# 128-row scores in the forgetting attention, and the low part of every weight formed on VectorE

## The chip, the cores and the metric

The program runs on one core of one Trainium2 chip. The metric is the device time of one execution in microseconds (us); lower is better. Engines are called by the profile's names: PE is TensorE's matmul, PEld its weight load, DVE is VectorE, ACT ScalarE, POOL GpSimd, SP the queue that starts most transfers.

## The reference

One sequence of 512 tokens with 1024 features goes through four layers, all in float32.

- **a**: RMS norm, then a mixer of two halves: a gated three-tap convolution (512 features), and *forgetting attention* with 8 heads of 64: softmax of `q k / 8 + C[t] - C[s]` over the keys s up to t, where C is the running sum of `log_sigmoid` of one gate value per head and token. Output projection, norm, residual, SwiGLU feed-forward (FFN, hidden size 2816), norm, residual.
- **b**: a conformer convolution module (pointwise, 31-tap depthwise, layer norm, SiLU, pointwise), then the same FFN.
- **c**: an HGRN2 mixer (gated linear recurrence, 8 heads of 128), then a FFN whose gate first passes a three-tap convolution.
- **d**: grouped-query attention over a window of 128 keys with sinks, 16 heads of 64, then the FFN with the convolution, and a final norm.

```
log_f = jax.nn.log_sigmoid((proj[..., OFF_F:] + b_f).astype(jnp.float32))
y_b = forgetting_attention(q, k, v, log_f).reshape(bsz, seq, D_FOX)
return jnp.concatenate([y_a, y_b.astype(h.dtype)], axis=-1) @ w_out
```

## The kernel before

Activations lie feature-major: 8 chunks of 128 features by 512 tokens. All weights come as 378 *slots* of 128x1024 float32 (512 KB) through a ring of 4 buffers (`RING`), in the order of `SLOT_PARTS`. A product is made of three matmuls in the float32r type (`product`): each weight and each activation is split into a high part, rounded to float32r, and a low part, the rest; high by high, high by low and low by high are added in PSUM. One slot is 8 products, so 24 matmuls of 512 columns.

For each slot: SP loads `raw` when the buffer is free (`slot_done` of the slot 4 before); ACT copies it to `w_hi` (`high_part`, called through `slot_over(s)`, which waits until slot s is done and makes the high part of slot s+3, as `AHEAD = 3`); POOL subtracts, `w_lo = raw - w_hi` (`low_part`, L396), and raises `w_ready`; PE waits for `w_ready` to reach the slot's number plus one. The low parts are made in slot order. POOL also does 6 of the 8 products of the four post-norms (`norm_output`), the blocks of depthwise taps (`tap_blocks`) and 3 chunks of the last norm; the low parts fill the rest of its list. Every engine works through its own list in order; semaphores are the only tie.

The places that matter here:

- **Start of a stage after a norm** (`a_pre`, `b_pre`, `c_pre`, and the four `*_fpre` at a FFN): PE runs `two_chunks` (slots s0, s0+1 at once, chunk by chunk as `u_lo` arrives), then slot s0+2, then `mean_square`, whose result ACT turns into `rs`, the factor by which all outputs of the stage are scaled (`rs_ready`), and without a wait for `rs` PE goes on with slot s0+3.
- **`norm_add`** on DVE (L1401, L1411, L1393) after the post-norms of layers a and b: residual adds `h`, low parts `u_lo` of the new inputs, then `sum_squares` (L1388).
- **`feed_forward`** on DVE, `pair(i, b)`: scale the gate output by `rs` (L1475), in layers c and d wait for ACT (L1047) and add two taps (L1485), then wait for the value slot and ACT's SiLU, multiply, scale, and split into `hid_hi` and `hid_lo`. One pair goes with two slots.
- **Forgetting attention** (`scores`, `attend`, L636 to L664): for each of 8 heads PE makes the scores of 4 query blocks, one or two slots of the gated convolution (`conv_slot`, 12 slots in 8 heads; even heads have one, odd heads two), all but the last two of the last slot's 8 products; then transposes of the probabilities, those last two products, and the values (plain float32, L662, a pass of 2 instructions each), whose output has 64 rows. Two heads share one bank, and ACT and DVE split it once for two heads. ACT's list per head: 4 exps, high parts, 4 copies of the transposes; DVE's: 4 maxima (L1560), reciprocal, 4 scalings (L1567), then the convolution's work.
- **Window attention** (layer d): scores have a 128-row contraction already, low and high part of a query in the two halves of the rows (`dq`). DVE's list per head pair: normalise (L1910), query low part (L1860), maxima (L1891), output low part, query evacuation, next pair's mask and add (L1881).

Of the kernel before, what the change touches and what calls it, by code (L numbers as in the profile page):

```python
# [5 lines left out]
F32 = mybir.dt.float32  # L6
# [6 lines left out]
P = 128  # L13
# [6 lines left out]
FOX_HEADS, FOX_DIM = 8, 64  # L20
HG_HEADS = 8
# [94 lines left out]
def build(nc, weights, vectors, squares, select_d, masks_d, x_t, out_t):  # L116
    with ExitStack() as ctx:
# [29 lines left out]
        with ExitStack() as fox:  # L147
            aq_hi = sb("aq_hi", [P, 4, T], F32R, fox)
            aq_lo = sb("aq_lo", [P, 4, T], F32R, fox)
            ak_hi = sb("ak_hi", [P, 4, T], F32R, fox)  # L150
            ak_lo = sb("ak_lo", [P, 4, T], F32R, fox)
            av = sb("av", [P, TT, 512], F32, fox)
            az = sb("az", [P, T + SHORT_TAPS - 1], F32, fox)
            agc = sb("agc", [P, T], F32, fox)
            ay = sb("ay", [P, T], F32, fox)
# [5 lines left out]
            ac = sb("ac", [FOX_HEADS, T], F32, fox)  # L161
# [3 lines left out]
            select = sb("select", [P, FOX_HEADS, P], F32R, fox)  # L165
# [48 lines left out]
        STAT, TOK_STAT = bank[4], bank[5]  # L214

# [54 lines left out]
        def rows_of(e):  # L270
            return slice(64 * e, 64 * e + 64)

# [120 lines left out]
        def _(pool):  # L393
            def low_part(s, j):
                pool.wait_ge(hi_ready, s + 1)
                pool.tensor_tensor(w_lo[:, j, :], raw[:, j, :], w_hi[:, j, :].bitcast(F32), ALU.subtract)\  # L396
                    .then_inc(w_ready, 1)

            def low_parts(a, b):

                if b - a >= RING:
                    with pool.Fori(0, (b - a) // RING) as i:
                        for n in range(RING):
                            low_part(RING * i + a + n, (a + n) % RING)
                for s in range(b - (b - a) % RING, b):
                    low_part(s, s % RING)

# [16 lines left out]
            pool.wait_ge(w_ready, DVE_SLOTS)  # L424
            low_parts(DVE_SLOTS, SLOT["a_ffn_in"] + AHEAD - 1)
            norm_output("a_post")
            low_parts(SLOT["a_ffn_in"] + AHEAD - 1, SLOT["b_in"] + AHEAD - 1)
            norm_output("a_fpost")
            low_parts(SLOT["b_in"] + AHEAD - 1, SLOT["b_in"] + AHEAD)

            pool.memset(bwv[:, :, :], 0.0).then_inc(taps_zeroed, 1)
            for n in range(2 * KC):
                s = SLOT["b_in"] + AHEAD + n
                low_part(s, s % RING)
                if n == 1:
                    pool.wait_ge(taps_landed, 16 * SHIFTS * (GROUPS + 1))
                if 1 <= n <= CONV_RING:
                    tap_blocks(n - 1)
                if n % 2 and n // 2 >= CONV_RING:
                    tap_blocks(n // 2)  # L440
            low_parts(SLOT["b_out"] + AHEAD, SLOT["b_ffn_in"] + AHEAD - 1)
            norm_output("b_post")
            low_parts(SLOT["b_ffn_in"] + AHEAD - 1, SLOT["c_fq"] + AHEAD - 1)
            norm_output("b_fpost")
            low_parts(SLOT["c_fq"] + AHEAD - 1, N_SLOTS)
# [7 lines left out]
        def _(pe):  # L453
# [184 lines left out]
            def scores(hd):  # L638
                r, c = slice(64 * (hd % 2), 64 * (hd % 2) + 64), hd // 2
                for qb in range(TT):  # L640
                    w = (qb + 1) * P
                    if hd > 0:
                        pe.wait_ge(pt_ready, 4 * hd)
                    s = bank[4 + qb]
                    product(s[:, 0:w], aq_hi[r, c, qb * P:w], aq_lo[r, c, qb * P:w], ak_hi[r, c, 0:w], ak_lo[r, c, 0:w],
                            True, False)
                    pe.matmul(s[:, 0:w], select[:, hd, :], ac2[:, 0:w], start=False, stop=False)  # L647
                    pe.matmul(s[:, qb * P:w], ident_r[:, :], causal[:, :], start=False, stop=True).then_inc(scores_ready, 1)

            def attend(hd, between):  # L650
                r = slice(64 * (hd % 2), 64 * (hd % 2) + 64)
# [12 lines left out]
                last.then_inc(o_ready, 1)  # L664
# [16 lines left out]
            pe.wait_ge(qkl_ready, 8)  # L681
# [9 lines left out]
            def fox_ready(k):  # L691
                if k < 4:
                    pe.wait_ge(u_ready, SPLIT["a_gate"] + k + 1)
                else:
                    pe.wait_ge(ol_ready, k - 3)
# [266 lines left out]
        def _(act):  # L962
# [136 lines left out]
            for dst, src in ((ident_r[:, :], ident), (causal[:, :], ap[:, 0, 0:P]), (select[:, :, :], select_raw)):  # L1099
# [3 lines left out]
            for n in range(8):  # L1103
# [3 lines left out]
                act.activation((aq_hi if n < 4 else ak_hi)[:, n % 4, :], ut[:, n % 2, :], ACT.Copy).then_inc(qkh_ready, 1)  # L1107
# [19 lines left out]
            for hd in range(FOX_HEADS):  # L1127
# [15 lines left out]
                for kt in range(TT):  # L1143
                    act.wait_ge(pt_full, 4 * hd + kt + 1)
                    after(act, o_ready, hd)
                    act.activation(apt[:, kt, kt * P:T], bank[4 + kt][:, kt * P:T], ACT.Copy).then_inc(pt_ready, 1)
                conv_over(slots[-1])
                if hd % 2:
                    act.wait_ge(o_ready, hd + 1)
                    act.activation(acat_hi[:, 4 + hd // 2, :], bank[3][:, :], ACT.Copy).then_inc(oh_ready, 1)  # L1150
# [219 lines left out]
        def _(dve):  # L1370
            def split_value(name, c, make):
# [58 lines left out]
            def keep_out(part, stat, bias=None):  # L1430
                for n in range(KC):
                    dve.wait_ge(slot_done, SLOT[part] + n + 1)
                    keep_chunk(stat, n, bank[n % 4], bias(n) if bias else None)

            def add_out(l):

                for n in range(KC + 1):
# [5 lines left out]
                    if n >= 2:  # L1443
                        sum_squares(f"{l}_fpre", (n - 1,))

            def add_ffn(l, stat, split=None):

                for half in range(2):
                    for n in range(4 * half, 4 * half + 4):
# [580 lines left out]
```

## Time and profile before

| | |
|---|---|
| median of 3 runs | 2493.75 us (2493.46 to 2494.15) |
| the profiled execution: its time | 2494.29 us |
| its span in the trace | 2492.5 us |
| mean granted PE clock | 0.983 of full |
| busy: PE, DVE, POOL, ACT | 2406.4, 1266.8, 1001.1, 822.3 us |
| POOL low parts (L396) | 376, 936.4 us |

The span is the stretch from the first to the last instruction; the time of an execution is 1.8 us longer. Busy time is the union of an engine's instructions; PE's matmuls overlap in it, since each is shown longer than the distance to the next one. A wait is named by the instruction that ended it.

### The profile page before, as it was taken

What the parts mean: (1) busy time and instruction counts of PE and PEld (TensorE: products, weight loads), DVE (VectorE), ACT (ScalarE), POOL (GpSimd) and SP (SyncE); (2) the same over time, 40 slices, a digit from 0 to 9 for tenths busy, and PEclk for the clock granted to TensorE, in tenths of its full rate; (3) what the DMA queues carried; (4) which work ended last, traced back from release to release, by engine and by line L of the source; (5) the groups of instructions that cost most, each with busy time, mean ns of one, the idle gap of its engine ahead of it and who ended that gap; (6) DMA issues with size and microseconds to landing.
All of it is one profiled execution on the core that took longest, in us unless ns stands there. A gap on an engine that the chain in (4) does not pass through costs nothing.

```text
span 2492.5 us, 30910 instructions
## 1 busy us (share of the span) xinstructions
PE 2406.4 (97%) x11202; PEld 1922.7 (77%) x11202; DVE 1266.8 (51%) x1590; ACT 822.3 (33%) x1194; POOL 1001.1 (40%) x416
## 2 busy tenths in 40 slices
PE   8999899999899889999989999999999979999997
PEld 6777688888664678888768888888888768888886
DVE  4453544411533464441166776577731796677701
ACT  5333422222321532222242254333322564332322
POOL 3223444444543344444443222454444313444543
PEclk9999999999899999999989999999999999999999
DMA  4112233333264223333322211333333212333332
GB/s 152 60 51 69 67 101 93 101 93 93 62 168 121 68 76 93 99 95 93 93 72 85 60 43 51 94 101 93 101 93 93 77 36 68 93 101 93 97 97 77
DMA packets 68001, 216.12 MB, mean 87 GB/s; under 512 B 11600, under 2 KB 12112, under 8 KB 67920
## 3 DMA queue, kind: packets, MB, share of 16 engines
q1 hardware_dynamic: 67632, 214.63, 28.8%
q8 instruction: 56, 0.92, 0.1%
q10 hardware_dynamic: 288, 0.36, 0.1%
q14 instruction: 25, 0.20, 0.0%
HBM read 210.64 MB, written 4.33 MB: 86 GB/s over the span
## 4 chain that ended last, share of the span: by engine, by line
PE 91%; DVE 5%; ACT 1%; issue 1%; POOL 1%; DMA 0%; DVEq 0%; SPq 0%; POOLq 0%
PE bank L456 28%; PE bank L457 27%; PE bank L458 27%; PE bank L718 2%; PE bank L811 2%; DVE ds L1910 1%; DVE h L1411 1%; DVE u_lo L1393 1%; PE bank L662 1%; ACT ds L1327 1%; PE bank L647 0%; DVE small L1891 0%; PE bank L655 0%; POOL m L413 0%; DVE dq L1860 0%
## 5 line engine op out<-in xcount | busy, mean ns | idle before, releaser
L396 POOL TENSOR_TENSOR w_lo<-raw,w_hi 128x1024 fp32r<-128x1024 f32 x376 | 936.4, 2496 | 1446.1 <-ACT w_hi L971 1446.0
L456 PE MATMUL bank<-u_hi,w_hi 128*128 128x512 f32 x1952 | 773.4, 396 | 19.1 <-DVE u_lo L1393 18.7
L457 PE MATMUL bank<-u_lo,w_hi 128*128 128x512 f32 x1952 | 766.2, 393 | 0.0
L458 PE MATMUL bank<-u_hi,w_lo 128*128 128x512 f32 x1952 | 765.9, 392 | 0.0
L971 ACT ACTIVATE w_hi<-raw 128x1024 fp32r<-128x1024 f32 x378 | 395.0, 1056 | 999.9 <-PE bank L458 929.9
L456 PEld LDWEIGHTS bank<-u_hi,w_hi 128*128 128x128 f32 x1952 | 370.8, 190 | 106.8 <-DVE u_lo L1393 23.6
L458 PEld LDWEIGHTS bank<-u_hi,w_lo 128*128 128x128 f32 x1952 | 370.4, 190 | 78.1
L457 PEld LDWEIGHTS bank<-u_lo,w_hi 128*128 128x128 f32 x1952 | 371.1, 190 | 76.6 <-issue 1.0
L456 PE MATMUL bank<-hid_hi,w_hi 128*128 (+1 forms) x704 | 278.1, 395 | 0.0
L458 PE MATMUL bank<-hid_hi,w_lo 128*128 (+1 forms) x704 | 278.1, 395 | 0.0
L457 PE MATMUL bank<-hid_lo,w_hi 128*128 (+1 forms) x704 | 278.1, 395 | 0.0
L1494 DVE TENSOR_SCALAR hid_hi<-ut 128x512 f32 (+1 forms) x88 | 203.2, 2309 | 11.8 <-DVE ut L1491 0.3
L1489 DVE TENSOR_TENSOR ut<-gconv,bank 128x512 f32<-128x512 f32 x88 | 60.6, 689 | 225.9 <-PE bank L458 190.8
L458 PEld LDWEIGHTS bank<-hid_hi,w_lo 128*128 128x128 f32 x704 | 132.0, 187 | 32.4
L456 PEld LDWEIGHTS bank<-hid_hi,w_hi 128*128 128x128 f32 x704 | 132.0, 187 | 32.3
L457 PEld LDWEIGHTS bank<-hid_lo,w_hi 128*128 128x128 f32 x704 | 132.0, 187 | 32.2
L1496 DVE TENSOR_TENSOR hid_lo<-ut,hid_hi 128x512 f32 (+1 forms) x88 | 140.3, 1595 | 10.1
L1426 DVE COPY m<-bank 128x512 f32<-128x512 f32 x24 | 16.5, 688 | 249.4 <-ACT sq L986 240.6
L1047 ACT ACTIVATE gconv<-ut,vec 128x512 f32<-128x512 f32 x44 | 36.0, 818 | 236.1 <-DVE ut L1475 236.1
L1451 DVE TENSOR_TENSOR h<-h,bank 128x512 f32<-128x512 f32 x16 | 11.0, 688 | 200.8 <-PE bank L458 200.2
L1485 DVE SCALAR_TENSOR_TENSOR gconv<-ut,vec,gconv 128x511 f32<-128x511 f32 x88 | 66.1, 751 | 55.2 <-ACT gconv L1047 49.3
L1388 DVE TENSOR_TENSOR acc<-acc,sq 128x512 f32<-128x512 f32 x73 | 77.9, 1067 | 7.6 <-ACT sq L986 4.6
(271 smaller groups left out, 2463.7 us busy)
## 6 DMA issues: line engine op xcount, KB each, us to landing
raw<-weights_dram SPq DMA_DIRECT2D x378, 512.0 KB, 3.5
bz<-gated_dram SPq DMA_DIRECT2D x32, 270.0 KB, 5.0
gated_dram<-bz SPq DMA_DIRECT2D x8, 272.0 KB, 2.1
h<-x_t_dram SPq DMA_DIRECT2D x8, 256.0 KB, 5.9
out_dram<-m SPq DMA_DIRECT2D x8, 256.0 KB, 2.2
ap<-select_dram SPq DMA_DIRECT2D x1, 512.0 KB, 8.7
vec<-vectors_dram SPq DMA_DIRECT2D x1, 343.0 KB, 7.7
cmask<-masks_dram ACTq DMA_DIRECT2D x1, 224.0 KB, 2.6
```

Of the source, the lines that this page charges most:

```text
L396: pool.tensor_tensor(w_lo[:, j, :], raw[:, j, :], w_hi[:, j, :].bitcast(F32), ALU.subtract)\
L456: pe.matmul(out, wh, xh, start=start, stop=False)
L457: pe.matmul(out, wh, xl, start=False, stop=False)
L458: return pe.matmul(out, wl, xh, start=False, stop=stop)
L718: last = pe.matmul(out[32 * g:32 * g + 32, :], bw[:, b, g * STEPS + q, :], bz4[:, b, g, SHIFTS * q:SHIFTS * q + T], start=(q == 0), stop=( ...
L811: last = pe.matmul(out, ck[:, hd, s], queries, start=True, stop=True)
L971: act.activation(w_hi[:, j, :], raw[:, j, :], ACT.Copy).then_inc(hi_ready, 1)
L1388: dve.tensor_tensor(acc[:, :], sq[:, 0, :] if c == 1 else acc[:, :], sq[:, c % 2, :], ALU.add).then_inc(acc_ready, 1)
L1485: dve.scalar_tensor_tensor(out=gconv[:, b, back:], in0=ut[:, b, 0:T - back], scalar=w, in1=gconv[:, b, back:], op0=ALU.mult, op1=ALU.add). ...
L1489: dve.tensor_tensor(ut[:, b, :], gconv[:, b, :], bank[2 * b + 1][:, :], ALU.mult).then_inc(ht_ready, 1)
L1494: dve.tensor_scalar(hi, ut[:, b, :], 1.0, None, ALU.mult).then_inc(hh_ready, 1)
L1496: dve.tensor_tensor(lo, ut[:, b, :], hi.bitcast(F32), ALU.subtract).then_inc(hid_ready, 1)
```

## The change

1. **Scores with 128 rows.** Before, a head's query and key parts (`aq_hi`, `aq_lo`, `ak_hi`, `ak_lo`) lay in 64 rows and the scores took three 64-row matmuls; the forget term (`select`) and the causal mask were two more of 128 rows. Now `aq` holds a head's high part in its own 64 rows and the low part in the other 64; `ak_hi` holds the high key part in both halves, and `ak_lo` the low key part in the head's rows and zeros in the others. Two 128-row matmuls give the three products. ACT makes 2 instead of 1 pieces for each query slot and 4 instead of 1 for each key slot, DVE 2 instead of 1, and DVE writes the zeros. `select` is one column per head, broadcast.
2. **Values in two halves of the rows.** The output of query blocks 0 and 3 goes to one half of the bank's rows, that of blocks 1 and 2 to the other (`FOX_HALVES`), 7 matmuls per head instead of 4. ACT and DVE now split each head's output in two pieces of 64 rows by 256, and the values of a head wait for the split of the head before.
3. **All low parts on DVE.** POOL makes none. DVE makes slots 0 to 2 at the start, and every later one in `low_over(s)` (slot s+3), at places in its own list.
4. `agc`, `ay`, `ac` take the memory of `sq` and `acc`.

```
-            def low_part(s, j):
-                pool.wait_ge(hi_ready, s + 1)
-                pool.tensor_tensor(w_lo[:, j, :], raw[:, j, :], w_hi[:, j, :].bitcast(F32), ALU.subtract)\
-                    .then_inc(w_ready, 1)
...
+            def low_part(s, i=0):
+                j = s % RING
+                dve.wait_ge(hi_ready, s + RING * i + 1)
+                dve.tensor_tensor(w_lo[:, j, :], raw[:, j, :], w_hi[:, j, :].bitcast(F32), ALU.subtract).then_inc(w_ready, 1)
+            def low_over(s, i=0):
+                if s + AHEAD < N_SLOTS:
+                    low_part(s + AHEAD, i)
...
scores(hd):
-                    product(s[:, 0:w], aq_hi[r, c, qb * P:w], aq_lo[r, c, qb * P:w], ak_hi[r, c, 0:w], ak_lo[r, c, 0:w],
-                            True, False)
-                    pe.matmul(s[:, 0:w], select[:, hd, :], ac2[:, 0:w], start=False, stop=False)
+                    pe.matmul(s[:, 0:w], aq[:, c, e, qb * P:w], ak_hi[:, c, e, 0:w], start=True, stop=False)
+                    pe.matmul(s[:, 0:w], aq[:, c, e, qb * P:w], ak_lo[:, c, e, 0:w], start=False, stop=False)
+                    pe.matmul(s[:, 0:w], select[:, hd:hd + 1].to_broadcast([P, P]), ac2[:, 0:w], start=False, stop=False)
...
attend(hd):
-                if hd % 2 == 0 and hd >= 2:
-                    pe.wait_ge(ol_ready, hd // 2)
+                if hd:
+                    pe.wait_ge(ol_ready, 2 * hd)
                 for kt in range(TT):
                     pe.wait_ge(pt_ready, 4 * hd + kt + 1)
-                    last = pe.matmul(bank[3][r, kt * P:T], av[:, kt, hd * FOX_DIM:(hd + 1) * FOX_DIM],
-                                     apt[:, kt, kt * P:T], start=(kt == 0), stop=(kt == TT - 1))
+                    for half, qbs in FOX_HALVES[kt]:
...
+                        last = pe.matmul(o, av[:, kt, hd * FOX_DIM:(hd + 1) * FOX_DIM], of, start=(kt == 0), stop=(kt == qbs[-1]))
...
DVE, keep_out (a_out, b_out) and add_out (c_out, d_out), after the work on chunk n:
+                    if n < KC - 1:
+                        low_over(SLOT[part] + n)
...
DVE, after norm_add, sum_squares included (the same before b_in, b_ffn_in and c_fq):
             norm_add("a_mix", "mix_post", 0, "a_fpre", "a_fpre")
+            low_over(SLOT["a_ffn_in"] - 1)
             feed_forward("a", None)
...
DVE, pair(i, b) of feed_forward, after the scaling by rs and the taps:
+                    low_over(s0 + 2 * b, i)
                     dve.wait_ge(slot_done, s0 + 2 * j + 2)
...
and after hid_lo:
+                    low_over(s0 + 2 * b + 1, i)
...
DVE, the loops over the slots of a_q and a_k, b_in and c_fq, behind the scaling of slot n by rs:
+                low_over(n)
...
DVE, forgetting attention, per head after each convolution slot's work, then the split of the output:
+                    low_over(SLOT["a_conv"] + n)
...
+                for i, ((_, h_), (_, l_), (r, src)) in enumerate(zip(halves_of(hi), halves_of(lo), halves_of(found))):
+                    dve.wait_ge(oh_ready, 2 * hd + i + 1)
+                    dve.tensor_tensor(l_, src[r], h_.bitcast(F32), ALU.subtract).then_inc(ol_ready, 1)
...
DVE, window attention: two before the first window_add, and in the loop over c, between window_probs and query_low:
+                    low_over(SLOT["d_q"] + c + 2)
```

In the HGRN2 part there is one `low_over` per level, in the conformer part one per slot, and `way_back` and `last_back` make those of a FFN's second matrix.

## Rows read from the trace of the kernel before

**Rows 1.** The profile page: span, busy time by engine, the chain by engine.

```profile
span 2492.5 us, 30910 instructions
PE 2406.4 (97%) x11202; PEld 1922.7 (77%) x11202; DVE 1266.8 (51%) x1590; ACT 822.3 (33%) x1194; POOL 1001.1 (40%) x416
...
PE 91%; DVE 5%; ACT 1%; issue 1%; POOL 1%; DMA 0%; DVEq 0%; SPq 0%; POOLq 0%
```

**Rows 2.** Groups of instructions by line: busy us, mean ns, idle before and releaser.

```profile
L396 POOL TENSOR_TENSOR w_lo<-raw,w_hi 128x1024 fp32r<-128x1024 f32 x376 | 936.4, 2496 | 1446.1 <-ACT w_hi L971 1446.0
```

**Rows 3.** Line 1517, low parts on DVE: min/median/max in ns.

```profile
L1517 DVE TENSOR_TENSOR w_lo<-raw,w_hi x2: 1225/1225/1225, 6.2 to 8.1; 128x1024 fp32r<-128x1024 f32 x2
```

**Rows 4.** Timeline of PE, values of head 1 and scores of head 2: start, us.

```profile
115.08 2.37 PE L662 MATMUL bank<-apt,av 128*64 128x512 f32 x8
...
117.38 0.32 PE L456 MATMUL bank<-ak_hi,aq_hi 64*128 64x128 f32 x1
...
121.17 0.19 PEld L647 LDWEIGHTS bank<-ac,select 128*128 128x128 f32 x1 [0.35 <-issue]
...
121.57 0.44 PE L456 MATMUL bank<-u_hi,w_hi 128*128 128x512 f32 x1
```

**Rows 5.** Timeline of PE in the window attention: first and last scores, values.

```profile
1973.63 0.30 PE L891 MATMUL bank<-dk_hi,dq 128*128 128x128 f32 x1 [3.24 <-DVE dq L1860]
...
1975.46 0.28 PE L892 MATMUL bank<-dk_lo,dq 128*128 128x256 f32 x1
...
1993.09 1.75 PE L915 MATMUL bank<-dpt,dv 128*64 128x128 f32 x28
```

**Rows 6.** The chain in order of time: transposes of heads 1 to 4.

```profile
112.66 1.09 PE bank L655 x10
...
125.91 1.09 PE bank L655 x10
...
144.57 1.09 PE bank L655 x10
...
159.36 1.09 PE bank L655 x10
```

**Rows 7.** Timeline of DVE, head 2: maxima of the last block, scalings.

```profile
121.77 0.69 DVE L1560 TENSOR_REDUCE small<-bank 128x1 f32<-128x512 f32 x1 [0.81 <-PE bank L648]
...
123.52 1.28 DVE L1567 TENSOR_SCALAR ap<-ap,small 128x128 f32<-128x128 f32 x4
```

**Rows 8.** Start of layer a's FFN: chain of PE, timelines of POOL, ACT, DVE.

```profile
293.10 0.86 PE bank L520 x2
...
291.85 4.83 POOL L396 TENSOR_TENSOR w_lo<-raw,w_hi 128x1024 fp32r<-128x1024 f32 x2 [0.36 <-ACT w_hi L971]
...
294.80 0.63 ACT L998 ACTIVATE rs<-rs 128x512 f32<-128x512 f32 x1
...
295.54 0.69 DVE L1475 TENSOR_TENSOR gconv<-bank,rs 128x512 f32<-128x512 f32 x1 [6.62 <-ACT rs L998]
```

**Rows 9.** Start of layer c's FFN: timelines of PE and DVE.

```profile
1596.07 1.02 PE L520 MATMUL bank<-acc,ones 128*128 128x512 f32 x2
...
1600.60 1.54 DVE L1485 SCALAR_TENSOR_TENSOR gconv<-ut,vec,gconv 128x511 f32<-128x511 f32 x2 [0.89 <-ACT gconv L1047]
```

**Rows 10.** Timelines of DVE and PE after layer b's post-norm.

```profile
879.86 2.85 DVE L1411 SCALAR_TENSOR_TENSOR h<-m,vec,h 128x512 f32<-128x512 f32 x1
...
891.29 4.67 DVE L1388 TENSOR_TENSOR acc<-acc,sq 128x512 f32<-128x512 f32 x6 [0.76 <-ACT sq L986]
...
897.21 1.02 PE L520 MATMUL bank<-acc,ones 128*128 128x512 f32 x2
```

**Rows 11.** Two stretches at the start of layer d: busy (count), granted PE clock.

```profile
1955.09:1958.50 3.41, 1.38 (x6) 1.07 (x6) 3.14 (x3) 3.41 (x7) 2.05 (x1) 0.98 0.71 288
1958.50:1961.92 3.42, 3.42 (x10) 2.67 (x9) 3.42 (x5) 3.26 (x5) 1.28 (x1) 0.52 0.00 0
```

**Rows 12.** Line 1910 between 1997 and 2003 us: min/median/max in ns.

```profile
L1910 DVE TENSOR_SCALAR ds<-ds,small x8: 282/340/2455, 1997.8 to 2001.7; 128x256 f32<-128x256 f32 x6, 128x128 f32<-128x128 f32 x2
```

More of the change, by code:

```diff
@@ L1502, in feed_forward, with way_back, last_back @@
                         pair(i, b)
-            def keep_ffn(l, stat):
-                for n in range(KC):
-                    keep_chunk(stat, n, ffn_full(dve, l, n))
+            def way_back(l, half):
+                s = SLOT[f"{l}_ffn_out"] + HALF * half
+                with dve.Fori(0, 2) as i:
+                    for n in range(RING):
+                        low_over(s + n, i)
+                for n in range(2 * RING, HALF - 1):
+                    low_over(s + n)
+            def last_back(l, half):
+                low_over(SLOT[f"{l}_ffn_out"] + HALF * (half + 1) - 1)
+            def keep_ffn(l, stat):
+                for half in range(2):
+                    way_back(l, half)
+                    for n in range(4 * half, 4 * half + 4):
+                        keep_chunk(stat, n, ffn_full(dve, l, n))
+                    if not half:
+                        last_back(l, half)
             dve.memset(ones[:, :], 1.0).then_inc(consts_made, 1)
@@ L1515, in _ @@
                 if c < DVE_SLOTS:
-                    dve.wait_ge(hi_ready, c + 1)
-                    dve.tensor_tensor(w_lo[:, c, :], raw[:, c, :], w_hi[:, c, :].bitcast(F32), ALU.subtract).then_inc(w_ready, 1)
+                    low_part(c)
                 scaled_low("a_pre", c)
+            for c in range(DVE_SLOTS, AHEAD):
+                low_part(c)
             sum_squares("a_pre")
@@ L1537, in _ @@
                     low_qk(n - 1)
+                low_over(n)
             low_qk(7)
+            for e in range(2):
+                none = ones[rows_of(1 - e), 0:1].unsqueeze(2).to_broadcast([64, 4, T])
+                dve.tensor_scalar(ak_lo[rows_of(1 - e), :, e, :], none, 0.0, None, ALU.mult).then_inc(qkl_ready, 1)
             f8 = slice(0, FOX_HEADS)
@@ L1554, in _ @@
             dve.tensor_tensor(ac2[LOW_ROW:LOW_ROW + FOX_HEADS, :], ac[:, :], ac2[f8, :].bitcast(F32), ALU.subtract).then_inc(c_low, 1)
+            for n in range(1, 4):
+                low_over(SLOT["a_v"] + n)
             nmax, rsum, rinv = small[:, 0:8], small[:, 8:16], small[:, 48:56]
@@ L1609, in _ @@
             norm_add("a_ffn", "ffn_post", 0, "b_pre", "b_pre")
+            low_over(SLOT["b_in"] - 1)
             dve.memset(bz[:, :, 0:LONG_TAPS - 1], 0.0)
@@ L1644, in _ @@
                     dve.tensor_tensor(ba[:, n // 2 % 2, n % 2, :], bank[n % 4][:, :], rs[:, :], ALU.mult).then_inc(b_evac, 1)
+                    if n % 2 == 0:
+                        low_over(SLOT["b_in"] + n)
                 elif what == "gated":
@@ L1652, in _ @@
                        .then_inc(bz_ready, 1)
+                    low_over(SLOT["b_in"] + 2 * n + 1)
                 elif n >= 1:
@@ L1688, in _ @@
             norm_add("b_ffn", "ffn_post", KC, "c_pre", "c_pre")
+            low_over(SLOT["c_fq"] - 1)
             l0, l1, e0, e1 = col("lb_logits", 0, KC), col("lb_logits", KC, KC), small[:, 16:24], small[:, 24:32]
@@ L1715, in _ @@
                        .then_inc(c_evac, 1)
+                    low_over(SLOT["c_fq"] + n)
                 if n == 0:
```

111 lines of the change are left out of this document (60 added, 51 removed).

## The prediction

> **What bounds the kernel now.** I read the page first: PE is busy 2406 of 2492.5 us and 91% of the chain of waits is PE, while DVE is busy half and POOL 40% of the time [rows 1]. So a microsecond counts only where PE waits, or where PE itself gets less to do. The groups by line come next. POOL's low parts take 2.50 us each, 936 us in all, and each of them waits for ACT's high part, not the other way round [rows 2]; PE never waits for them but once, for 0.3 us, at a FFN start (a small group of the waits). To move them is worth nothing by itself: the question is whether DVE has them ready in time, at each place of its list. Then I read the timelines of the stretches in which PE depends on DVE: stage starts, forgetting attention, HGRN2, window attention. In the long loops a slot takes PE 24 x 0.227 = 5.44 us, so a pair of the FFN takes 10.9 us; DVE's own work there with two low parts of 1.23 us [rows 3] is about 5.6 us in layers a and b and 7.2 us in c and d. The low part of slot s+3 has two slots of time. DVE doesn't become the bound of the loops, and nothing is gained there either, since PE's distance of 0.227 us between matmuls is the same whether POOL works beside it or not.
>
> **Forgetting attention: scores.** A head's scores take from 117.38 to 121.57, 4.2 us [rows 4], for 20 matmuls of 128 to 512 columns. The 64-row and the 128-row ones alternate, and at the change the weight load of `select` stands idle for 0.35 us with nothing to wait for [rows 4]. After the change there are 16, all of 128 rows. The window attention's scores are such: 16 matmuls from 1973.63 to 1975.46, 0.12 us apart at 256 columns [rows 5]. With 0.11, 0.12, 0.17 and 0.23 us for the four widths, three per block and a mask matmul of 0.11, and 0.06 us where the width grows: 3 x 0.63 + 0.44 + 0.24 = 2.6 us. Saved: 1.6 us a head, 13 us in all. The lower end is the removed matmul alone, 0.63 x 8 = 5 us; the upper 15. I take 13, since the window attention's row is the same kind of matmul. By the Trainium skill, TensorEngine Tiling (Array Packing), section Key Properties, a change of tiling mode drains the array, which would explain the idle 0.35 us; by a plain count of matmuls the saving would be 5 us, by that rule 13.
>
> **Values.** Four float32 matmuls (8 instructions) take 2.3 us, 1280 columns [rows 4]. Packed in two halves of the rows, the same work is ten blocks of 128 columns, five in each half. In the window attention, 14 such blocks in alternating halves take 1.75 us [rows 5], 0.25 us for two: five times that and 0.1 us are 1.35 us. Saved 0.95 us a head, 7.6 us in all (0 if the halves don't run side by side, 9 at most).
>
> **What the softmax chain gives back.** From head 1's transposes to head 2's pass 13.25 us, to head 3's 18.7, to head 4's 14.8 [rows 6]. The 1.5 us extra of head 4, and some 0.9 us in head 0, are stretches at the half clock; I expect them to go, as the sparse matmuls that stand before them do. With one slot between them (heads 2, 4, 6), DVE has to do the following after the last slot: gate product, its low part (waiting for ACT), a low part of weights (done 3.5 us after the slot), two pieces of output (4.4 us; new in front of the maxima), maxima until 6.1, exps and reciprocal 1.1, scalings 1.28 [rows 7]: 8.5 us. PE wants them after 0.35 + 1.35 + 2.6 + 4.1 = 8.4 us. So the slack that is there now (scalings end 124.80, transposes at 125.91 [rows 6, 7]) is gone, and I count 0.2 us of waiting for three heads and 0.5 us in head 0, where ACT's copies of `av` come first. Forgetting attention in sum: 13 + 7.6 + 2.4 - 1.1 = 22 us less. The doubled ACT and DVE pieces of queries and keys lie under slots (ACT 3.6 us of 5.4); the zeros cost DVE 2.6 us before the gate's chain, which has some 12 us to spare.
>
> **Stage starts: where the low part is late.** PE runs slot s0+3 directly behind `mean_square`. Its low part comes from POOL now, ahead of time: POOL makes two from 291.85 on [rows 8]. After the change it is `low_over(s0)`, which DVE does after scaling the first output by `rs`, and `rs` comes out of `mean_square`. So PE must stand. Layer a: PE would go on at 293.10 + 0.86 = 293.96; ACT has `rs` at 295.43, DVE scales from 295.54 to 296.23 [rows 8], the low part takes 1.23: 297.5, a wait of 3.5 us. The same holds for b's FFN and for `b_in`; at `a_q` and `c_fq`, 0.8 us of small matmuls follow `mean_square`, so 2.7 each. In the FFNs of c and d the low part also stands behind ACT's and DVE's taps, which end at 1602.14; 1603.4 against 1596.93 is 6.4 us each [rows 9]. Sum: 10.5 + 5.4 + 12.8 = 28.7 us. If DVE starts the low part later than ACT's other work allows it is up to 2 us more at each; it can't be less, since the order in DVE's list forces it.
>
> **The slot before it.** After the post-norms, slot s0+2 gets its low part after `sum_squares` instead of on POOL. Layer b: the squares end at 895.96; the DVE instruction that POOL's low part holds up now (2.85 us, its neighbours 0.74) gives back 2.1; then 1.23: 895.1, and PE asks at 897.21 - 5.44 = 891.8 [rows 10]. 3.3 us late. At a's FFN, `b_in` and `c_fq`, PE comes later (longer at the half clock), and the same sum gives 0.4 to 0.9. In all 5.2 us, less the 0.3 us that PE waited for POOL in layer b. With no low part late it would be 0. After `c_out` and `d_out`, the low part comes 3.4 us after the last slot, and PE has 10.9.
>
> **Window attention and HGRN2.** Each of six rounds is bound by DVE, and in each, one scaling takes 2.46 instead of 0.34 us while POOL works [rows 12]. That goes, a low part comes: 1.2 - 2.1, six times -0.95 = -5.7 us. Two more low parts stand before the first `window_add` (+2.4) but the input's low parts aren't held up any more (eight in 9.1 us where 5.3 do), and PE starts 1.2 us sooner: together -0.3. In HGRN2 a level takes PE 9.0 us and DVE 7.6 with its low part; one wait of 0.5 us goes. Sum -6.5 us.
>
> **Sum at the full clock.** -22 + 28.7 + 5.2 - 0.3 - 6.5 = +5.1 us.
>
> **The clock.** At the start of layer d PE stands for 2.0 us (busy 1.38 of 3.41), and in the next 3.4 us the granted clock is 0.52, the lower of the two levels, 1.2 GHz: 10 matmuls where 17 go at the full clock, 1.6 us lost [rows 11]. The new waits of 2.7 us and more are eight: five stage starts of 2.7 to 3.5, b's slot s0+2 with 3.3, and two of 6.4 us. After a whole stretch of standing there are two or three such stretches now, some of them idle anyway: I take 3.0 us for each of the two, and 1.3 us on the mean for the other six, as one that falls across two stretches may do nothing: 14 us. Bounds: 0, and 25. The Trainium skill, TensorE: Matmul & The Clock Gate, section HAM oscillation — how this bites in real kernels, says that repeated waits bring the clock down each time anew: by it, each new wait would cost more than its length; the trace agrees at this one place.
>
> The profiled execution took 2494.3 us, so 2494.3 + 5.1 + 14 = 2513.4; the median of the runs is 0.5 us lower: **2513 us**. Differences of 0.2% (5 us) are about what a measurement of this kernel can tell from none.
>
> **Rivals.**
> - *The waits come, the clock stays up.* 2494 + 5 = 2499. For it: rounds of the window attention with waits of 1.6 us don't lower the clock. Against it: [rows 11]. Chance 0.15, half of it within 0.2%.
> - *The low parts are not late* (the other side). If DVE reached the low part of slot s0+3 before PE asks, the 28.7 and 5.2 us and the clock's 14 would be gone: 2494 - 22 - 7 = 2465. It turns to faster once waits and clock together cost less than 24 us. Against it: `rs_ready` stands before `pair(0, 0)` and PE's values slot waits on the count. For it: only that the order of small things in a list is easily misread. With gains at their upper ends, 0.08.
> - *The softmax chain becomes the bound in each head*: DVE is 2 us later than I count in the heads with one slot and PE waits there, the clock with it: 8 us more, 2521. Chance 0.10.
> - *The two halves of the values run one after another*: 7.6 us less gain, 2521. Against it: rows of layer d. Chance 0.07.
> - The likeliest, 0.60: 2505 to 2520.
>
> The range 2496 to 2526 takes in all but the second rival, and the ends of clock and scores. Faster by over 0.2%: 0.08; within: 0.10; slower: 0.82.
>
> **What will show it.** PE idle of about 3.5 us behind each `mean_square` of a stage start, released by DVE's `w_lo`, 6.4 in c and d; in layer b also one slot earlier. No POOL low parts, `w_lo` on DVE at 1.23 us x376. Heads' transposes 10.9 us apart for one slot, 16.1 for two. Scaling at L1910 all at 0.3 us, rounds of 11.9 instead of 12.8 us. More stretches at half clock. I would be wrong if the waits are there but short, if PE finds `w_lo` ready, or if the clock doesn't follow.

## The result: slower by 1.2%, and the profile after

| | before | after |
|---|---|---|
| median of the runs, us | 2493.95 | 2526.85 |
| least and greatest, us | 2493.46, 2499.97 | 2522.76, 2528.06 |
| profiled execution, its span, us | 2494.29, 2492.5 | 2528.06, 2526.1 |

The ratio, that of the means (2526.1 and 2495.3 us), is 1.0123, with a 95% interval from 1.0107 to 1.0139. One of the four executions of `e3_early_both`, further on, took 2854.2 us at a mean granted clock of 0.787, and its ratio leaves that one out. The forecast was 2513 us: the sign is right, the loss is 33 us where 19 were forecast, and the median lies 0.9 us above the upper end of the range.

The page of the changed kernel, its first part, its chain, and two of its groups (against [rows 1, 2, 3]):

```profile
span 2526.1 us, 30717 instructions
PE 2401.5 (95%) x11218; PEld 1925.9 (76%) x11218; DVE 1342.2 (53%) x1988; ACT 837.4 (33%) x1222; POOL 62.9 (2%) x40
...
PE 87%; DVE 8%; ACT 3%; issue 1%; DMA 0%; DVEq 0%; SPq 0%; ACTq 0%
...
L430 PE MATMUL bank<-u_hi,w_hi 128*128 128x512 f32 x1952 | 779.5, 399 | 61.8 <-DVE w_lo L1359 44.2
...
L1359 DVE TENSOR_TENSOR w_lo<-raw,w_hi 128x1024 fp32r<-128x1024 f32 x378 | 463.3, 1226 | 380.8 <-ACT w_hi L948 380.2
```

DVE makes a low part in 1.23 us where POOL took 2.50, and DVE is still busy only 53% of the time. Yet PE's share of the chain fell from 91 to 87%. The new line is the releaser of the first group: PE stood 44.2 us, eleven times by the waits, for low parts.

The stretches below are cut at the same PE instructions in each kernel's trace (us; the last two columns are experiments told further on, `e4_early_s3` and `e3_early_both`):

| stretch | before | after | after, slot s0+3 early | after, s0+2 and s0+3 early |
|---|---|---|---|---|
| start to the transposes of head 0 | 93.8 | 99.1 | 93.2 | 93.0 |
| heads 0 to 7 | 115.9 | 96.9 | 96.9 | 96.9 |
| to a's post-norm | 48.9 | 48.7 | 48.7 | 48.7 |
| a's FFN | 382.5 | 389.6 | 385.7 | 379.5 |
| `b_in`, long convolution, `b_out` | 224.4 | 237.6 | 230.7 | 225.9 |
| b's FFN | 380.4 | 390.5 | 384.5 | 378.9 |
| `c_fq` | 106.4 | 114.8 | 110.0 | 103.5 |
| HGRN2 | 227.4 | 226.6 | 226.6 | 226.6 |
| c's FFN and window attention | 534.1 | 536.3 | 529.4 | 529.3 |
| d's FFN | 364.8 | 372.3 | 366.4 | 366.4 |
| tail | 13.6 | 13.6 | 13.6 | 13.6 |

The heads won 19 us; everything with a stage start in it lost. Within the span the clock records have 10 stretches at the lower level (1.2 GHz) before, 83.6 us in all, and 19 of them after, 124.4 us.

Here is the start of layer a's FFN in the changed kernel, the timeline of ACT, DVE and PE (start, length, and in brackets how long the engine stood and for whom); it answers to [rows 8]:

```profile
281.23 1.02 PE L494 MATMUL bank<-acc,ones 128*128 128x512 f32 x2
...
283.10 0.63 ACT L975 ACTIVATE rs<-rs 128x512 f32<-128x512 f32 x1
...
283.83 0.69 DVE L1476 TENSOR_TENSOR gconv<-bank,rs 128x512 f32<-128x512 f32 x1 [9.86 <-ACT rs L975]
284.43 1.22 DVE L1359 TENSOR_TENSOR w_lo<-raw,w_hi 128x1024 fp32r<-128x1024 f32 x1
...
285.70 0.79 PE L430 MATMUL bank<-u_hi,w_hi 128*128 128x512 f32 x1 [3.45 <-DVE w_lo L1359]
```

DVE stood idle for 9.86 us in front of the scaling, while the low part that PE needed next was behind it in the list. That is the forecast wait, 3.5 us. It is followed by a stretch at the half clock; at the start of layer c's FFN the same is seen by stretches (busy of PE first, its granted clock third from the end):

```profile
1620.00:1623.40 3.40, 0.92 (x3) 0.09 (x1) 0.69 (x1) 2.44 (x4) 0.00 (x0) 1.00 0.53 154
1623.40:1630.20 6.80, 3.40 (x8) 2.76 (x9) 5.99 (x8) 2.55 (x3) 0.00 (x0) 0.50 0.00 0
1630.20:1633.60 3.40, 3.40 (x16) 2.82 (x16) 0.79 (x2) 0.00 (x0) 0.00 (x0) 0.99 0.00 0
```

PE is busy 0.92 us of 3.4, then 3.4 of 6.8 at a granted clock of 0.50. In these 3.4 busy us it has eight matmuls, and in the 3.4 us afterwards, at 0.99, it has 16.

The largest new wait had only 0.4 to 0.9 us in my sum. It is in front of slot s0+2 of `b_in` (DVE, POOL, PE):

```profile
657.78 7.91 DVE L1383 TENSOR_TENSOR acc<-acc,sq 128x512 f32<-128x512 f32 x6 [0.76 <-ACT sq L963]
665.62 2.98 DVE L1359 TENSOR_TENSOR w_lo<-raw,w_hi 128x1024 fp32r<-128x1024 f32 x1
...
660.81 6.70 POOL L410 TENSOR_TENSOR bw<-bwv,eye 128x1024 f32<-128x1024 f32 x3 [12.58 <-DMA bwv<-vectors_dram]
...
668.65 0.79 PE L430 MATMUL bank<-u_hi,w_hi 128*128 128x512 f32 x1 [7.72 <-DVE w_lo L1359]
```

The six additions take 4.67 us at every other stage start, and 7.91 here; the low part 2.98 instead of 1.22. POOL, which has no low parts between its tap blocks any more, makes three blocks in a row in just these microseconds.

### The profile page after: what moved, and what is told of

It is laid out like the page before. It is cut to its first block, busy times and chain, and to the rows that moved or that the text cites. A ratio compares the mean times of both kernels' runs of the same rounds, so it can differ in the third digit from the quotient of the medians.

```text
span 2526.1 us, 30717 instructions
## 1 busy us (share of the span) xinstructions
PE 2401.5 (95%) x11218; PEld 1925.9 (76%) x11218; DVE 1342.2 (53%) x1988; ACT 837.4 (33%) x1222; POOL 62.9 (2%) x40
## 4 chain that ended last, share of the span: by engine, by line
PE 87%; DVE 8%; ACT 3%; issue 1%; DMA 0%; DVEq 0%; SPq 0%; ACTq 0%
PE bank L430 27%; PE bank L432 26%; PE bank L431 26%; PE bank L788 2%; PE bank L695 2%; DVE h L1406 1%; DVE u_lo L1388 1%; DVE w_lo L1359 1%; ACT ds L1311 1%; DVE acc L1383 1%; DVE small L1944 1%; DVE ds L1963 1%; ACT w_hi L948 1%; DVE dq L1911 0%; DVE m L1396 0%
## 5 line engine op out<-in xcount | busy, mean ns | idle before, releaser
L430 PE MATMUL bank<-u_hi,w_hi 128*128 128x512 f32 x1952 | 779.5, 399 | 61.8 <-DVE w_lo L1359 44.2
L1359 DVE TENSOR_TENSOR w_lo<-raw,w_hi 128x1024 fp32r<-128x1024 f32 x378 | 463.3, 1226 | 380.8 <-ACT w_hi L948 380.2
L1027 ACT ACTIVATE gconv<-gconv 128x512 f32<-128x512 f32 x88 | 54.9, 624 | 76.8 <-DVE gconv L1486 76.8
L1476 DVE TENSOR_TENSOR ut<-bank,rs 128x512 f32<-128x512 f32 x44 | 30.4, 691 | 82.9 <-PE bank L432 54.1
L1476 DVE TENSOR_TENSOR gconv<-bank,rs 128x512 f32<-128x512 f32 x44 | 30.4, 691 | 77.0 <-PE bank L432 56.2
L401 POOL TENSOR_TENSOR m<-m,rs 128x512 f32<-128x512 f32 x24 | 40.7, 1728 | 1100.8 <-ACT rs L975 1100.8
L989 ACT ACTIVATE u_hi<-h,vec 128x512 fp32r<-128x512 f32 x72 | 50.4, 717 | 49.8 <-DVE h L1406 43.2
L1498 DVE TENSOR_TENSOR hid_lo<-ut,hid_hi 128x512 f32 (+1 forms) x88 | 61.0, 693 | 10.1
```

Of the source, the lines that this page charges most:

```text
L430: pe.matmul(out, wh, xh, start=start, stop=False)
L1027: act.activation(gconv[:, b, :], gconv[:, b, :], ACT.Silu).then_inc(gate_ready, 1)
L1359: dve.tensor_tensor(w_lo[:, j, :], raw[:, j, :], w_hi[:, j, :].bitcast(F32), ALU.subtract).then_inc(w_ready, 1)
L1476: dve.tensor_tensor(scaled[:, b, :], bank[2 * b][:, :], rs[:, :], ALU.mult).then_inc(scaled_ready, 1)
L1498: dve.tensor_tensor(lo, ut[:, b, :], hi.bitcast(F32), ALU.subtract).then_inc(hid_ready, 1)
```

## The experiments

Times are medians; each is compared with runs of the kernel before on the same chip (2495.0 to 2495.5 us in the three sets, so about 1.5 us above the first). "Theory" is that of the prediction: the two parts of the change are nearly independent, and the loss is one of place in DVE's list, plus the clock.

**One part alone.** `e1_fox_only` has the changed forgetting attention, and POOL makes the low parts as before:

```
             def low_over(s, i=0):
-                if s + AHEAD < N_SLOTS:
-                    low_part(s + AHEAD, i)
+                pass
...
+            pool.wait_ge(w_ready, DVE_SLOTS)
+            low_parts(DVE_SLOTS, SLOT["a_ffn_in"] + AHEAD - 1)
...
```

POOL's list is that of the kernel before from there on.

> The forgetting attention as changed, the low parts of the weights left on POOL as before. My theory (the two parts are nearly independent; the heads gain by shorter scores, shorter value products and the half-clock stretches that go): the stretch from the first to the last head's transposes loses 19 us, and the start loses nothing, so 2473 to 2478 us against 2494 of before. Rival A (the heads gained only because the low parts left POOL, with this part worth its count of matmuls alone, about 5 us): 2487 to 2491. If the start of the kernel is still some 4 us later than before, the extra instructions of the changed queries and keys are to blame for it and not the low parts.

Measured: 2476.9 us, ratio 0.992 (0.9897 to 0.9943). The time lies in the theory's range. The heads take 98.8 us against 115.9, 17.1 less where 19 were expected, and the start 92.7 against 93.8. So the extra pieces of queries and keys are not what makes the start of the whole change late (99.1 us); with the low parts made early there (`e4_early_s3`) it is 93.2.

`e2_low_only` is the kernel before with the low parts on DVE (the diff's other half).

> The forgetting attention as before, all low parts on DVE. If the parts add, this costs what the whole change cost plus what the first part gained: 2526 + 19 = 2545 us, 2541 to 2549. Rival (the low parts on DVE collide with the head loop, where DVE has the softmax to do, only together with the longer list of the changed attention): under 2535, with e1_fox_only near before's time plus a few us.

Measured: 2549.7 us, 1.0211 (1.0191 to 1.023), 0.7 us above the expected range. In the medians the parts nearly add: -18.6 and +54.2 give +35.7, and both together cost 32.9. By the profiled spans (2477.7 and 2547.4) they miss by 6.5 us. In the old heads the low parts on DVE cost 5 us (120.7 against 115.9), with three stretches at the half clock where there was one; in the new ones they gain 2 (98.8 to 96.9), which makes 6.7. The start goes the other way, by 5.0: it takes 95.3 us here and 99.1 in the whole change, with the same wait of 2.73 us in `a_q`, but no stretch at the half clock behind it. The rest is spread over the other stretches, at most 2.2 us in one of them.

**Another place in the list.** `e4_early_s3` makes the low parts of slots s0+3 and s0+4 before DVE waits for `rs`, at all seven stage starts. The diff for the FFNs; `a_q`, `b_in` and `c_fq` alike:

```
                     else:
+                        if b == 0:
+                            low_over(s0)
+                            low_over(s0 + 1)
                         dve.wait_ge(rs_ready, RS[f"{l}_fpre"] + 1)
...
-                    low_over(s0 + 2 * b, i)
+                    if b or not isinstance(i, int):
+                        low_over(s0 + 2 * b, i)
...
-                    low_over(s0 + 2 * b + 1, i)
+                    if b or not isinstance(i, int):
+                        low_over(s0 + 2 * b + 1, i)
```

`e3_early_both` has that and, in `norm_add`, slot s0+2's as well:

```
                     elif c >= DVE_NORMS:
                         scaled_low(split, c - 1)
+                    if c == 2:
+                        low_over(last)
                 sum_squares(stat)
```

> As e3_early_both, but only slots s0+3 and s0+4 are made early; slot s0+2 stays behind the sum of squares. Theory: 28 us of waits and some 10 us of half clock come back, 2486 to 2492 us, and the difference to e3_early_both sizes the late slot s0+2 (6 to 9 us, and the clock that follows). Rival 'DVE's load': 2508 or more.

> The whole change, but DVE makes the first two low parts of each stage (slots s0+3 and s0+4) before it waits for the norm's factor, and the last one of the stage before (slot s0+2) inside the norm's additions, before the sum of squares. DVE's amount of work is unchanged. Theory 'place in DVE's list': the waits for a late low part at the starts go, 28 us for slot s0+3 in seven stages and 6 to 9 for slot s0+2, and with them most of the extra half-clock stretches (12 to 16 us): 2474 to 2484 us. The 7.7 us wait at the start of b_in is the uncertain one: if it comes from DVE slowed by POOL's tap blocks, it stays in part. Rival 'DVE's load' (whatever the place, the 1.2 us per slot lands on a chain that ends at PE, as the scaling or the sum of squares is then later by as much): at most half of it comes back, 2500 us or more.

Measured: `e4_early_s3` 2487.3 us, 0.9962 (0.995 to 0.9975); `e3_early_both` 2464.4 us, 0.987 (0.9848 to 0.9892), better than the theory's range by 10 us. Spans: 2526.1, 2485.6, 2462.3. The rival "DVE's load" is out: DVE's busy time is 1342 to 1343 us in all three. The same place in `e3_early_both` (DVE):

```profile
263.20 4.67 DVE L1383 TENSOR_TENSOR acc<-acc,sq 128x512 f32<-128x512 f32 x6 [0.76 <-ACT sq L963]
268.06 2.36 DVE L1359 TENSOR_TENSOR w_lo<-raw,w_hi 128x1024 fp32r<-128x1024 f32 x2 [0.18 <-ACT w_hi L948]
272.65 0.69 DVE L1481 TENSOR_TENSOR gconv<-bank,rs 128x512 f32<-128x512 f32 x1 [2.23 <-ACT rs L975]
```

Two low parts fit into the time in which DVE stood for `rs`, and 2.2 us are left over. By the table the late slot s0+3 cost 40.5 us and the late slot s0+2 another 23.3. That second number is more than four times my term of 5.2 us in the prediction, and more than the 6 to 9 us of waits, with the clock that follows, in the expectation.

**POOL's tap blocks.** `e6_taps_late` is the whole change, with POOL's tap blocks held to their old places:

```
-            for c in range(KC):
-                tap_blocks(c)
+            for n in range(2 * KC):
+                pool.wait_ge(hi_ready, SLOT["b_in"] + AHEAD + n + 1)
+                if 1 <= n <= CONV_RING:
+                    tap_blocks(n - 1)
+                if n % 2 and n // 2 >= CONV_RING:
+                    tap_blocks(n // 2)
```

> The whole change, but POOL makes the tap blocks of the long convolution when the high parts of the weights reach the places that they had in the order before (it waits for them; it does no other work more). What it tests: in the changed kernel DVE's sum of squares and a low part took 5.0 us longer at the start of b_in, beside POOL's tap blocks, and PE waited 7.7 us there. Theory 'POOL's tap blocks slow DVE': the stretch from the post-norm of layer a's FFN to that of layer b's mixer falls from 237.6 to 231 to 233 us, the whole to 2520 to 2522. Rival 'the place of the low part alone': within 1.5 us of 237.6, as with the low parts made early the same stretch took 225.9 us although POOL's tap blocks were as early.

Measured: 2523.1 us, 1.0105 (1.0088 to 1.0121), 1.1 us above the expected 2520 to 2522. The stretch takes 231.8 us (the profiled span is 2520.8), inside the theory's 231 to 233, where the rival had 236.1 or more. The same rows there (DVE, then POOL):

```profile
657.08 4.67 DVE L1387 TENSOR_TENSOR acc<-acc,sq 128x512 f32<-128x512 f32 x6 [0.76 <-ACT sq L967]
661.67 1.22 DVE L1363 TENSOR_TENSOR w_lo<-raw,w_hi 128x1024 fp32r<-128x1024 f32 x1
...
664.49 1.97 POOL L410 TENSOR_TENSOR bw<-bwv,eye 128x1024 f32<-128x1024 f32 x1 [16.95 <-ACT w_hi L952]
```

DVE's two groups are back at their usual lengths. `e7_all_early` puts this together with `e3_early_both`.

> As e3_early_both, with POOL's tap blocks late as in e6_taps_late. e3_early_both took 2464 us, and its stretch with b_in 225.9 us against 224.4 of the kernel before. If the tap blocks still cost something there, 1.5 us less: 2462 to 2464. If they are hidden, the same as e3_early_both within 1 us.

Measured: 2460.2 us, 0.9856 (0.9839 to 0.9872). I had expected at most 1.5 us, since the stretch was near that of before already; it fell by 5.9, from 225.9 to 220.0 us. The main reason is in `e3_early_both` (DVE, POOL, PE):

```profile
642.67 9.46 DVE L1383 TENSOR_TENSOR acc<-acc,sq 128x512 f32<-128x512 f32 x6 [0.76 <-ACT sq L963]
...
644.27 7.31 POOL L410 TENSOR_TENSOR bw<-bwv,eye 128x1024 f32<-128x1024 f32 x3 [12.28 <-DMA bwv<-vectors_dram]
...
652.18 1.12 PE L494 MATMUL bank<-acc,ones 128*128 128x512 f32 x2 [2.75 <-DVE acc L1383]
```

With the low part out of the way the sum of squares itself was the thing that POOL made late, and PE's `mean_square` waited for it. That makes 2.9 us with a wait of 0.12 us behind it. The clock records of the stretch have 20.5 us at the half clock in `e3_early_both` and 13.7 in `e7_all_early`: 3.4 us of the difference lie right behind this wait, the other 3.4 at about 800 us, past the last tap block, so part of the 5.9 is likely chance. That I had judged by a stretch's sum, in which a gain and a loss had met, was the error of that expectation.

**The clock.** `e8_warm` leaves the low parts as late as they are and fills PE's waits at the four FFN starts:

```
                 mean_square(f"{l}_fpre")
+                keep_warm(s0 + 2, 13 if l in "ab" else 24)
                 values(0, 1)
```

> The whole change, and PE multiplies the high part of the slot before into an unused bank behind the mean square of each FFN start: 13 matmuls in layers a and b, 24 in c and d, 3.0 and 5.5 us, where it stands now for 3.5, 3.7, 5.9 and 5.9 us. The output isn't touched. Theory 'the waits bring the clock down, and half of the loss is the clock': the waits for the low part stay, filled with matmuls, and of the half-clock stretches behind these four waits (3.4, 10.2, 6.8 and 6.8 us, together 27 us) most go: 8 to 13 us less, 2513 to 2519 us. Rival 'the length of the waits alone': no change, within 3 us of 2526. If the matmuls run over the waits, each start is up to 0.5 us later.

Measured: 2518.6 us, 1.009 (1.0073 to 1.0107), 8.3 us less than the change, at the lower end of the theory. In layer a (PE):

```profile
281.59 3.56 PE L510 MATMUL bank<-w_hi 128*128 128x512 f32 x13
...
285.62 0.50 PE L430 MATMUL bank<-u_hi,w_hi 128*128 128x512 f32 x1 [0.47 <-DVE w_lo L1360]
```

The slot starts at 285.62 instead of 285.70, 4.5 us after the start of `mean_square` in both, but its first matmul takes 0.50 us instead of 0.79. No stretch at the lower clock follows any of the four waits now. The stretches of a, b, c and d became 1.4, 2.2, 2.4 and 1.3 us shorter, 7.3 in all. So that much of the loss was the clock and not the wait. The sum is safer than its parts: in `e6_taps_late`, whose lists are those of the change in these four stretches, b's took 0.65 and d's 0.9 us longer than in the change.

**Scores and values apart.** `e9_scores_only`: low parts on POOL, the value products as before.

> Of the forgetting attention's change only the 128-row scores (with their queries, keys and the narrow select), the value products and the low parts of the weights as before. Both parts together took 17 to 18.5 us off (e1_fox_only). My terms: scores 13 us, values 7.6, clock 2.4: 2479 to 2483 us. Rival (a plain count of the matmuls that go from the scores, 5 us, the rest from the value products): 2486 to 2490.

Measured: 2479.0 us, 0.993 (0.9913 to 0.9946), at the lower end of what my terms give. The distance between the transposes of heads with two slots between them is 18.66 us before, 16.9 with the scores alone, 15.9 with both: 1.75 us for a head's scores and 1.0 for its values. The removed matmul of each block is 0.63 of the 1.75. Where the rest was shows in the first block of head 2 before and of head 1 in the changed kernel (PE):

```profile
117.54 0.27 PE L457 MATMUL bank<-ak_lo,aq_hi 64*128 64x128 f32 x1
117.65 0.27 PE L458 MATMUL bank<-ak_hi,aq_lo 64*128 64x128 f32 x1
117.85 0.33 PE L647 MATMUL bank<-ac,select 128*128 128x128 f32 x1
...
103.10 0.27 PE L620 MATMUL bank<-ak_lo,aq 128*128 128x128 f32 x1
103.21 0.27 PE L621 MATMUL bank<-ac,select 128*128 128x128 f32 x1
```

Behind a matmul of the same number of rows the next starts after 0.11 us; from 64 to 128 rows it took 0.20, and there were eight changes between 64 and 128 rows in a head's scores. The values (in the kernel before [rows 4], 2.37 us) are in the changed kernel, for the same ten blocks of 128 columns:

```profile
101.70 1.30 PE L639 MATMUL bank<-apt,av 128*64 128x256 f32 x14
```

With one slot between them it is 13.25, 11.47, and then 11.76, longer again. There the softmax chain ends last. In `e1_fox_only`, head 2 (DVE, then PE):

```profile
112.79 2.46 DVE L1402 TENSOR_TENSOR acat_lo<-ut,acat_hi 128x512 fp32r<-128x512 f32 x1 [0.92 <-ACT acat_hi L1027]
...
120.25 1.31 PE L656 MATMUL bank<-identity,ap 128*128 128x128 f32 x10 [1.22 <-DVE ap L1621]
```

and in the changed kernel:

```profile
119.24 0.69 DVE L1375 TENSOR_TENSOR acat_lo<-ut,acat_hi 128x512 fp32r<-128x512 f32 x1 [0.92 <-ACT acat_hi L999]
119.85 1.22 DVE L1359 TENSOR_TENSOR w_lo<-raw,w_hi 128x1024 fp32r<-128x1024 f32 x1
...
126.08 1.31 PE L628 MATMUL bank<-identity,ap 128*128 128x128 f32 x10 [0.60 <-DVE ap L1601]
```

One subtraction takes 2.46 us while POOL makes its low part. Taking the low part over costs DVE 1.22 us and gives it back 1.8, so PE waits 0.6 us instead of 1.2.

**What the window attention gains.** `e11_window_only` is `e1_fox_only` with ten low parts on DVE:

```
-                pass
+                if SLOT["d_kv"] <= s < SLOT["d_out"]:
+                    if s == SLOT["d_kv"]:
+                        dve.wait_ge(w_ready, SLOT["d_kv"] + AHEAD)
+                    low_part(s + AHEAD, i)
```

> e1_fox_only (2477 us: new forgetting attention, low parts on POOL), but the ten low parts that fall into the window attention are DVE's. It sizes what DVE gains there when POOL is quiet. By my term for the window attention (0.95 us in each of six rounds and 0.3 beside it) the stretch from the start of layer c's FFN to that of layer d loses 6 us: 2470 to 2472 us. Rival (the shorter rounds came from DVE's low parts pulling work forward elsewhere, and POOL's effect on the scaling is no more than seen at one instruction): 2475 or more. If it comes out above e7_all_early (2460), DVE's low parts in the right places are worth more than these ten.

Measured: 2470.0 us, 0.9898 (0.9883 to 0.9913). The stretch went from 535.7 to 527.8 us, 7.8 less, where 6 were expected, with 13.7 us at the half clock in both. The rounds take 11.8 us instead of 12.8, as forecast. In the changed kernel line L1963 (before: [rows 12]) has no long instruction left:

```profile
L1963 DVE TENSOR_SCALAR ds<-ds,small x8: 278/348/350, 2029.1 to 2030.8; 128x256 f32<-128x256 f32 x6, 128x128 f32<-128x128 f32 x2
```

**The last wait.** `e7_all_early` still has this at the start of layer d's FFN (PE):

```profile
2107.62 0.50 PE L434 MATMUL bank<-u_hi,w_hi 128*128 128x512 f32 x1 [1.28 <-DVE w_lo L1363]
```

`e10_third_early` makes slot s0+5's low part behind the first scaling:

```
                     dve.tensor_tensor(scaled[:, b, :], bank[2 * b][:, :], rs[:, :], ALU.mult).then_inc(scaled_ready, 1)
+                    if isinstance(i, int) and b == 0:
+                        low_over(s0 + 2)
...
-                    if b or not isinstance(i, int):
+                    if not isinstance(i, int):
                         low_over(s0 + 2 * b, i)
```

> e7_all_early, and the third low part of each FFN (slot s0+5) is made right behind the first scaling, where DVE stands still anyway for ACT's taps or Silu. In e7_all_early PE waited 1.3 us for that slot at the start of layer d's FFN, and layer c's looks the same. Theory: these two waits go, 2.5 us, 2457 to 2458.5 against 2460.2. Rival (the low part now delays the first gate product, and PE waits for that instead): 2460 or more.

Measured: 2458.1 us, 0.9851 (0.9837 to 0.9864); d's stretch 364.8 instead of 366.4, c's 528.8 instead of 529.3. Both waits of 1.28 us are gone. It is the best version: 1.5% faster than before and 2.7% faster than the change, with the same work on every engine as the change, in another order.

## Why the prediction was right in sign and short in size

Point by point, by the steps of the prediction:

- **What bounds the kernel**: right. `e3_early_both` and the change have the same DVE work, and 64 us between their spans. DVE's load made no difference here, its order did.
- **Scores**: 13 us forecast; 1.75 us a head measured, 14 in eight heads. The 16 matmuls of a head's scores start from 102.93 to 105.28 us in the changed kernel, where 2.6 us were forecast for them. The plain count of the removed matmuls (5 us) is excluded by `e9_scores_only`. The Trainium skill, TensorEngine Tiling (Array Packing), section Key Properties, has the drain at a change of tiling mode. It gives no size; the matmuls that start 0.20 us after the one before, instead of 0.11, where 64 rows change to 128 agree with it. `e9_scores_only` takes the changes of mode and four matmuls a head away together, so the split of the 1.75 us into 0.63 and the rest is read from the rows.
- **Values**: 0.95 us a head forecast, 1.0 measured in the heads with two slots. The two halves do run side by side: 1.30 us where it was 2.37.
- **Softmax chain**: forecast 0.2 us of waiting in three heads and 0.5 in head 0; measured 0.6 in three heads, and PE stood 1.1 us for ACT's copies of `av` before head 0. The distances were forecast as 10.9 and 16.1 us; they are 11.1 and 15.9. No stretch at the half clock is left between the heads. From head 0 to head 7 that makes 19.0 us.
- **Slot s0+3**: right in each place. The waits are 2.73 (`a_q`), 3.45 (a), 3.38 (`b_in`), 3.45 (b), 2.79 (`c_fq`), 5.87 (c) and 5.87 us (d), 27.5 in all against 28.7.
- **The clock**: with it the late slot s0+3 cost 40.5 us by `e4_early_s3`, which leaves 13 for the clock and what hangs on it. `e8_warm` gives 7.3 us of it back at four of the seven places, 1.3 to 2.4 at each, where 1.3 to 3.0 were forecast. The first rival, that the clock stays up, is out. The Trainium skill, TensorE: Matmul & The Clock Gate, section HAM oscillation — how this bites in real kernels, describes this, a wait and then a cold start each time; the rows of a and c agree. At one start chance had a hand: the wait of 2.73 us in `a_q` is followed by 6.8 us at the half clock in the changed kernel, in `e6_taps_late` and in `e8_warm`, and by none in `e2_low_only`, with the same wait.
- **The slot before it: this step failed.** It was to cost 5.2 us; the waits are 2.48 (a), 7.72 (`b_in`), 3.71 (b) and 2.71 (`c_fq`), 16.6 us, and with the clock 23.3 by the two early versions. Two things were wrong in it.
  First, I took the times at which PE asks from the trace of before, in the stages with a long stretch at the half clock. Count from PE's first product behind its wait for `u_lo` (272.94 in a, 879.99 in b). DVE ends the low part 15.0 to 15.1 us after it in a, b and `c_fq`, in the changed kernel as in my sum. PE asked 14.6 us after it in a (287.5) and 11.8 in b, since the half clock lasted 10.2 us in a and 6.8 in b, and I wrote that PE comes later there. In the changed kernel it asks after 12.6, 11.4 and 12.3 us: a second stand of 0.5 us (at 276.38), and with it part of the slow stretch, has gone (6.8 us instead of 10.2 in a, 10.2 instead of 13.7 at `c_fq`). So b came out as forecast, 3.3 against 3.7 us, and a and `c_fq` at 2.5 and 2.7 instead of 0.4 to 0.9. The other runs show whose low parts make the difference. In the four kernels in which POOL makes them (before, `e1_fox_only`, `e9_scores_only`, `e11_window_only`), all 16 of these starts have the stand of 0.5 us, and in 14 the half clock lasts until 8.5 to 9.5 us after the first product. In the eight in which DVE makes them, none of 32 has it, and the half clock ends after 3.0 to 5.9 us. Layer b before, from which I took the 3.3 us, is one of the two starts with POOL where it ended early (3.2 us), so that b came out as forecast is luck. How POOL's low part makes the stand, by holding DVE up [rows 10], is read from the order of events.
  Second, of POOL I had only counted what it no longer does. What remains on it, the tap blocks, moved forward beside them: 5.0 us, on DVE's sum of squares and the one low part that PE was waiting for (it ends 20.1 us after the first product instead of 15.1, and PE asks after 12.3). `e6_taps_late` gives 5.8 us of its stretch back.
- **Window attention and HGRN2**: 6.5 us forecast; 7.8 in `e11_window_only` for the first, 0.8 for the second in the table.
- **What lay beside the sum**: the start is 5.3 us later. Of that 2.7 are the wait, which is in the sum, and 1.0 is PE's first product, which is not: it comes at 10.44 us instead of 9.45, by which other kernels differ too (9.34 in `e2_low_only`, 10.32 in `e1_fox_only`). The 1.6 us left are about what the clock would make: 6.8 us of half clock in that stretch against 3.4 before, an estimate of 1.7 us.

Sum, in spans: the heads -19.0, all that is left beside them and the late slots -11.2 (window attention and HGRN2, and the shorter slow stretches at the stage starts), slot s0+2 +23.3, slot s0+3 +40.5: +33.6 us. The prediction has -22, -6.5, +4.9 and +28.7, and 14 for the clock. The first pair is 1.7 us off in sum, the last two with their clock are 63.8 against 47.6: the late slot s0+2, with 23.3 us where 4.9 and one share of 1.3 of the clock stood, is 17 us off, more than the whole shortfall. So the mechanism was right, and the size of one term was not. The second rival, that the low parts aren't late, had 2465 us; the order that makes it true took 2464.4.

## What to carry to other kernels

When cheap work moves into the list of an engine that executes in order, its cost isn't its length but what it stands behind: put it in front of every wait whose release depends on the consumer, here a norm's factor, and check each stage start, since the steady loop will look perfect. The time at which an engine asks, read from a trace, holds the clock that it had there: work a lateness out at the full clock too, and take the worse. And ask of the engine that is relieved what its remaining work moves forward onto.

## What the runs showed of the hardware

- POOL's and DVE's instructions in SBUF hold each other up. Six additions of 0.69 us took 4.67 us undisturbed, 7.91 and 9.46 beside three POOL instructions of 2.0 to 2.5 us; these took 1.97 us alone. Each addition beside one of them took 2.3 us. A subtraction took 2.46 us instead of 0.69, and a `tensor_scalar` 2.46 instead of 0.34. The Trainium skill, SBUF — State Buffer, section SBUF: two separate sides, calls the shared port pair an exclusive lock; the rows agree. I hadn't expected that a mostly idle POOL (2% busy) could still cost 5.8 us, being busy in the wrong 6.7 us.
- Filling four waits of 3.4 to 5.9 us with matmuls that nobody needs was worth 7.3 us in their stretches, 1.3 to 2.4 us at each, though PE went on no earlier.
- Which stretches run at the lower clock isn't the same from kernel to kernel where the waits are: the post-norm of layer a is followed by 10.2 us at the half clock before, 6.8 after, 10.2 in `e3_early_both`, and 6.8 in `e7_all_early` against 10.2 in `e10_third_early`, which are the same up to there. Differences of 1 to 2 us in a single stretch can be that alone; the steps above rest on the sums and on larger ones.
